# Four places for block 1's compressed rows, and the next pair's second scores, shift and exponential a round sooner

## The chip, the cores and the metric

The kernel runs on one core of a Trainium2 chip. The metric is the device time of one execution in microseconds. Three executions of the kernel before took 2794.94, 2795.05 and 2795.95 us, median 2795.05.

## What is computed

Three transformer blocks run one after the other on 512 tokens of width 1024, all in fp32 (large products are made of two or three products of split operands). Only block 1 is touched: a sparse attention of 16 heads of 64, with three branches, of which this is the part that matters (cut from the reference):

```python
s_c = jnp.einsum('bgrqd,bgnd->bgrqn', qb, k_c).astype(jnp.float32) * scale
p_c = masked_softmax(s_c, c_end[None, :] <= tpos[:, None])
o_c = jnp.einsum('bgrqn,bgnd->bgrqd', p_c.astype(dt), v_c)
...
p_s = masked_softmax(s_s, m_s[:, :, None])
o_s = jnp.einsum('bgrqk,bgqkd->bgrqd', p_s.astype(dt), vs_g)
...
p_w = masked_softmax(s_w, m_w)
o_w = jnp.einsum('bgrqk,bgkd->bgrqd', p_w.astype(dt), vw)
return gb[..., 0:1] * o_c + gb[..., 1:2] * o_s + gb[..., 2:3] * o_w
```

The compressed branch (`s_c`, `p_c`) has 31 keys, so a head has 512 x 31 scores. With 512 tokens the selected and the window branch see all causal keys. The compressed keys come from two small weight matrices, `cw2k` being the second of them (128 x 256 in SBUF), which is used once before the attention.

## The kernel before

TensorE, VectorE, ScalarE, GpSimd and SyncE each have a program written out by hand; they meet at semaphores. Each engine's order of work is that of its program.

The attention of block 1 is one loop of 64 rounds. `head_and_tile(n)` gives round n's head (n // 8 * 2 + n % 2) and its tile of 128 queries (n % 8 // 2): eight rounds make a pair of heads, tiles 0 to 3, the two heads in turn. With m = n // 8, rounds 8m to 8m+7 work on heads 2m and 2m+1, and the compressed rows of heads 2m+2 and 2m+3 are prepared beside them.

TensorE in round n (main loop at L2926): `gate_filler(n)`, three 512-column matmuls for the attention gate (rounds 0 to 47; L2585 to L2587); `scores(n + 1)` (L2856 to L2858), which waits until the exponentials two rounds back are done and, where n % 8 == 5, for `c_shifted`; in rounds 8m and 8m+2 `compressed_scores` of heads 2m+2 and 2m+3 (L2865 the mask, L2868 eight matmuls of 32 columns) into a part of bank 5, waiting for `c_shifted >= h`, that is until the shift of the head before is done; in odd rounds `values(n - 3)` (L2907) for two rounds at once; `transposes(n - 1)` (L2894, and L2891 for the compressed rows where the tile is 0), which waits for the scaled rows and for the copies of the transposes before.

VectorE in round n: `keep_second_pt(n - 2)` copies one branch's transposed rows out of PSUM (L1941) once `tr_done` says they are there; `row_factor(n)` (L1931, L1932) after the exponentials of round n; `maxima(n + 1)` (L1925) after scores(n + 1); in rounds 8m+1 and 8m+3 `compressed_shift` of heads 2m+2 and 2m+3 (a row maximum, L1952, and a subtraction into the compressed rows, L1955); in rounds 8m+4 and 8m+6 `compressed_sum` (L1960 to L1963); once a pair `keep_heads` (L1967).

ScalarE in round n: `keep_pt(n - 2)` copies the other branch's transposed rows (L991, L993); `scale_rows(n)` (L983); in rounds 8m+2 and 8m+4 `compressed_exp` (L997); `exps(n + 1)` (L974); and once a pair, in round 8m+2, the cast of a weight unit (`split_hi`, L589).

GpSimd does taps of the convolution beside the loop (L464 to L469) and the low halves of weight units (L442).

The compressed rows (`PC_ROWS`, seen as `PC`) have two places, one for even and one for odd heads, each of 128 columns: four tiles of 31 scores and one column of zero, cleared once at the start. So the subtraction of head h waits until the rows of head h - 2 have been transposed.

Of the kernel before, what the change touches and what calls it, by code (L numbers as in the profile page):

```python
# [126 lines left out]
def build(nc, t, out, blocks=(1, 2, 3)):  # L127
    ctx = ExitStack()
    FIRST, COUNT, LAST, n_units = plan(blocks)
    with ctx:  # L130
# [119 lines left out]
        CW2K = region(2 * P).rearrange("p (c d) -> p c d", c=2)  # L250
        CW2V = region(2 * DH).rearrange("p (c d) -> p c d", c=2)
        CST = region(4)
# [313 lines left out]
        def _(a):  # L566
# [253 lines left out]
            def block_1():  # L820
# [174 lines left out]
                def compressed_exp(h):  # L995
                    a.wait_ge(c_shifted, h + 1)
                    a.activation(PC[:, h % 2, :, 0:NCMP], PC[:, h % 2, :, 0:NCMP], ACT.Exp).then_inc(c_exp, 1)  # L997
# [5 lines left out]
                for n in range(N + 2):  # L1003
# [6 lines left out]
                    if n % 8 in (2, 4) and n // 8 + 1 < NH // 2:  # L1010
                        compressed_exp(n // 8 * 2 + 2 + (n % 8 == 4))
# [473 lines left out]
        def _(v):  # L1485
            c = Count()

            def link(ins):

                ins.then_inc(dve_step, 1)  # L1490
                v.wait_ge(dve_step, c.add("step"))
# [255 lines left out]
            def block_1():  # L1747
# [199 lines left out]
                def compressed_shift(h):  # L1947

                    v.wait_ge(c_scores, h + 1)
                    at = h % 2 * TT * NC2  # L1950
                    sc = bank[5][:, at:at + TT * NC2].rearrange("p (q n) -> p q n", q=TT)[:, :, 0:NCMP]
                    link(v.tensor_reduce(CST, sc, AX.X, ALU.max))  # L1952
                    if h >= 2:
                        v.wait_ge(tr_done, (h // 2 - 1) * 8 + h % 2 + 1)
                    v.tensor_tensor(PC[:, h % 2, :, 0:NCMP], sc, per_row(CST), ALU.subtract).then_inc(c_shifted, 1)  # L1955

                def compressed_sum(h):
                    to, rows = CMP_FACTOR[:, h % 2], PC[:, h % 2, :, 0:NCMP]
# [20 lines left out]
                for n in range(N + 3):  # L1979
# [6 lines left out]
                    if n // 8 + 1 < NH // 2:  # L1986
                        if n % 8 in (1, 3):
                            compressed_shift(n // 8 * 2 + 2 + (n % 8 == 3))
                        if n % 8 in (4, 6):
                            compressed_sum(n // 8 * 2 + 2 + (n % 8 == 6))  # L1990
# [589 lines left out]
        def _(pe):  # L2580
# [183 lines left out]
            def block_1():  # L2764
# [117 lines left out]
                def transposes(n):  # L2882
# [6 lines left out]
                    if qt == 0:  # L2889
                        pe.wait_ge(c_scaled, h + 1)  # L2890
                        pe.transpose(bank[0][:, P:2 * P], PC_ROWS[:, h % 2], ident)  # L2891
# [34 lines left out]
                for n in range(N + 2):  # L2926
# [4 lines left out]
                    if n % 8 in (0, 2) and n // 8 + 1 < NH // 2:  # L2931
                        compressed_scores(n // 8 * 2 + 2 + (n % 8 == 2))
# [597 lines left out]
```

## Time and profile before

| | us |
|---|---|
| median of three runs | 2795.05 |
| profiled execution, its own time | 2790.86 |
| its span | 2789.1 |
| TensorE busy in the span | 2678.1 (96%) |
| TensorE weight loads | 2195.5 (79%) |
| VectorE busy | 1568.5 (56%) |
| ScalarE busy | 1056.2 (38%) |
| GpSimd busy | 1179.2 (42%) |

All times in the rows are microseconds from the span's start unless marked ns. A timeline row gives its start, its length, the engine, the line, the operation, the result and its operands, and in brackets how long the engine was idle before it and what ended that. Matmuls are pipelined: the listed length is longer than the distance between two starts. The loop of 64 rounds lies between about 275 and 498 us. The granted clock of TensorE is given as a share of 2.4 GHz, its mean over the span is 0.988.

### The profile page before, as it was taken

How to read it: one execution, taken by the hardware profiler on the slowest of the kernel's cores; microseconds unless marked ns; L12 is line 12 of the kernel's file. 1: busy time of each engine (PE TensorE's matmuls, PEld its weight loads, DVE VectorE, ACT ScalarE, POOL GpSimd, SP SyncE). 2: the span in 40 equal slices, each digit the busy share in tenths (PEclk: the TensorE clock that was granted, in tenths of full speed). 3: DMA queues.
4: the chain of work that ended last, by engine and by line, in shares of the span. 5: the costliest groups of instructions: out<-in, count | busy, mean ns of one | idle time of the engine just before them, and what ended most of it. 6: DMA issues, size and time to landing. Idle time of an engine off the chain costs nothing.

```text
span 2789.1 us, 38071 instructions
## 1 busy us (share of the span) xinstructions
PE 2678.1 (96%) x13128; PEld 2195.5 (79%) x13128; DVE 1568.5 (56%) x2448; ACT 1056.2 (38%) x1826; POOL 1179.2 (42%) x592
## 2 busy tenths in 40 slices
PE   8999888999999999999999999999899999999998
PEld 6877777778888878888887788888687778888886
DVE  8996666564342476476656735545623446653364
ACT  4224878623222254443324411112525553211133
POOL 3432595334444444354333344444442224444443
PEclk9999999999999999999999999999999999999999
DMA  3342000233322232221112332222231112322332
GB/s 137 99 140 83 16 24 9 65 131 100 98 98 92 96 131 84 82 94 61 54 38 95 134 98 95 94 98 95 97 104 56 46 45 91 128 97 92 98 98 90
DMA packets 67459, 242.88 MB, mean 87 GB/s; under 512 B 7771, under 2 KB 10116, under 8 KB 66572
## 3 DMA queue, kind: packets, MB, share of 16 engines
q1 hardware_dynamic: 59760, 215.37, 23.7%
q10 hardware_dynamic: 7580, 25.91, 2.7%
q8 instruction: 77, 1.26, 0.2%
q14 instruction: 42, 0.34, 0.0%
HBM read 232.80 MB, written 6.35 MB: 86 GB/s over the span
## 4 chain that ended last, share of the span: by engine, by line
issue 50%; PE 29%; POOL 18%; DVE 1%; ACT 1%; POOLq 1%; DVEq 0%; ACTq 0%
POOL w_lo L442 14%; PE bank L2585 7%; PE bank L2587 7%; PE bank L2586 7%; POOL stat L469 3%; PE bank L3133 2%; PE bank L3122 2%; POOL stat L466 2%; PE bank L2800 1%; POOLq L446 0%; PE bank L2771 0%; PE bank L3106 0%; PE bank L3171 0%; PE bank L3157 0%; PE bank L3109 0%
## 5 line engine op out<-in xcount | busy, mean ns | idle before, releaser
L442 POOL TENSOR_TENSOR w_lo<-raw,w_hi 128x1024 fp32r<-128x1024 f32 x398 | 972.7, 2444 | 1541.7 <-ACT w_hi L589 1420.7
L2585 PE MATMUL bank<-act,w_hi 128*128 128x512 f32 x3128 | 1259.6, 403 | 51.1 <-POOL w_lo L442 15.2
L2587 PE MATMUL bank<-act,w_lo 128*128 128x512 f32 x3128 | 1227.5, 392 | 0.0
L2586 PE MATMUL bank<-act,w_hi 128*128 128x512 f32 x3128 | 1226.3, 392 | 0.0
L589 ACT CAST w_hi<-raw 128x1024 fp32r<-128x1024 f32 x396 | 415.7, 1050 | 898.0 <-PE bank L2587 887.4
L2585 PEld LDWEIGHTS bank<-act,w_hi 128*128 128x128 f32 x3128 | 592.2, 189 | 198.7 <-issue 32.5
L2587 PEld LDWEIGHTS bank<-act,w_lo 128*128 128x128 f32 x3128 | 592.1, 189 | 127.2
L2586 PEld LDWEIGHTS bank<-act,w_hi 128*128 128x128 f32 x3128 | 593.0, 190 | 121.3 <-issue 5.7
L1685 DVE TENSOR_TENSOR X<-X,bank 128x512 f32 x56 | 38.5, 687 | 241.3 <-PE bank L2587 241.3
L2076 DVE CAST act<-tmp 128x512 f32 x64 | 142.5, 2226 | 10.0 <-DVE tmp L2072 5.2
L1837 DVE SCALAR_TENSOR_TENSOR bank<-big,cols,bank 128x512 f32<-128x512 f32 x174 | 117.1, 749 | 0.4
L2907 PE MATMUL bank<-big 128*64 128x128 f32 x768 | 50.7, 283 | 28.7 <-ACT big L991 18.6
L469 POOL TENSOR_TENSOR stat<-stat 128x512 f32<-128x512 f32 x58 | 74.5, 1285 | 4.8
L1732 DVE TENSOR_TENSOR tmp<-bank,stat 128x512 f32<-128x512 f32 x22 | 15.2, 692 | 104.9 <-PE bank L2587 104.9
L2907 PEld LDWEIGHTS bank<-big 128*64 128x64 f32 x768 | 43.0, 140 | 36.4 <-ACT big L991 23.9
L2476 DVE SCALAR_TENSOR_TENSOR big<-bank,stat 128x128 f32<-128x128 f32 (+3 forms) x32 | 15.7, 491 | 92.7 <-ACT stat L1410 92.7
L2251 DVE TENSOR_TENSOR stat<-bank,cst 128x256 f32<-128x256 f32 x96 | 40.7, 425 | 40.4 <-PE bank L3122 38.7
L1713 DVE TENSOR_TENSOR X<-X,bank 128x512 f32<-128x512 f32 x24 | 16.5, 688 | 80.4 <-PE bank L2587 73.9
L3122 PEld LDWEIGHTS bank<-big 128*128 128x128 f32 x384 | 51.2, 194 | 12.3 <-ACT big L1220 4.2
L3122 PE MATMUL bank<-big 128*128 128x128 f32 x384 | 54.2, 282 | 5.5 <-DVE big L2219 3.2
L1925 DVE TENSOR_REDUCE big<-bank 128x2 f32<-128x256 f32 (+3 forms) x64 | 52.5, 820 | 8.8 <-PE bank L2858 7.7
L753 ACT ACTIVATE tmp<-tmp 128x512 f32<-128x512 f32 x24 | 15.2, 631 | 109.0 <-DVE tmp L1729 109.0
(427 smaller groups left out, 2957.6 us busy)
## 6 DMA issues: line engine op xcount, KB each, us to landing
raw<-in_w_dram SPq DMA_DIRECT2D x402, 512.0 KB, 3.4
act_f<-head_rows ACTq DMA_DIRECT2D x8, 768.0 KB, 4.4
proj_rows<-big ACTq DMA_DIRECT2D x4, 1024.0 KB
big<-proj_rows ACTq DMA_DIRECT2D x2, 2048.0 KB, 9.0
X<-in_x_dram SPq DMA_DIRECT2D x4, 512.0 KB, 6.1
act_f<-in_cw1k_dram ACTq DMA_DIRECT2D x4, 512.0 KB, 4.3
cst<-in_consts_dram ACTq DMA_DIRECT2D x2, 648.5 KB, 7.7
X<-big ACTq DMA_DIRECT2D x8, 128.0 KB, 4.0
```

What stands on the lines that cost most here:

```text
L442: pool.tensor_tensor(w_lo[:, u], raw[:, u].rearrange("p (k n) -> p k n", k=KT), w_hi[:, u].bitcast(F32), ALU.subtract).then_inc(w_lo_ready, 1)
L466: pool.tensor_scalar(product, src, w, Z[:, k, 0:1], ALU.mult, ALU.add).then_inc(pool_step, 1)
L469: pool.tensor_tensor(to, acc, product, ALU.add).then_inc(done, 1)
L589: a.copy(w_hi[:, u].rearrange("p k n -> p (k n)"), raw[:, u]).then_inc(w_hi_ready, 1)
L1837: v.scalar_tensor_tensor(acc, src, w, acc, ALU.mult, ALU.add).then_inc(conv_tap, 1)
L2076: v.tensor_copy(hi, y).then_inc(hi_made, 1)
L2585: pe.matmul(o, l_hi, r_hi, start=start, stop=False)
L2586: pe.matmul(o, l_hi, r_lo, start=False, stop=False)
L2587: return pe.matmul(o, l_lo, r_hi, start=False, stop=stop)
L2907: ins = pe.matmul(bank[7][x * DH:x * DH + DH, qt * P:qt * P + P], v_rows, p_cols(x), start=start, stop=stop, tile_position=(0, x * DH), sk ...
L3122: ins = pe.matmul(bank[2 + half][:, quad[j]], MT[:, 2 * half + j], TM[:, 2 * half + j], start=True, stop=True)
L3133: ins = pe.matmul(bank[4 + half][:, quad[j]], XM[:, 2 * half + j], UM[h % 2][:, 2 * half + j], start=True, stop=True)
```

## The change

The compressed rows get four places instead of two: the two of `PC_ROWS` and the two halves of `CW2K`, whose weights have been used by then. Head h uses place h % 4. The zero column of the two new places is cleared by VectorE in the shifts of heads 2 and 3. The subtraction's wait on `tr_done` now concerns head h - 4 and exists from head 4 on.

The second head of the next pair (2m+3) moves: its `compressed_scores` from round 8m+2 to 8m+1 on TensorE, its `compressed_shift` from round 8m+3 to 8m+2 on VectorE, its `compressed_exp` from round 8m+4 to 8m+3 on ScalarE. Its `compressed_sum` stays in round 8m+6, and all of the first head's steps stay in their rounds. The wait of `compressed_scores(h)` for `c_shifted >= h` is as it was.

```diff
--- before.py
+++ after.py
@@ -248,7 +248,13 @@
             return tmp[:, 2 * (n % 3) + j] if n % 3 < 2 else ROWS_3[:, j]
 
         CW2K = region(2 * P).rearrange("p (c d) -> p c d", c=2)
+        PC_ROWS = (PC_ROWS[:, 0], PC_ROWS[:, 1], CW2K[:, 0], CW2K[:, 1])
         CW2V = region(2 * DH).rearrange("p (c d) -> p c d", c=2)
+
+        def compressed_rows(h):
+
+            return PC_ROWS[h % 4].rearrange("p (q n) -> p q n", q=TT)[:, :, 0:NCMP]
+
         CST = region(4)
         CMP_FACTOR = region(8).rearrange("p (b q) -> p b q", b=2)
         MX = region(4).rearrange("p (b k) -> p b k", b=2)
@@ -994,7 +1000,7 @@
 
                 def compressed_exp(h):
                     a.wait_ge(c_shifted, h + 1)
-                    a.activation(PC[:, h % 2, :, 0:NCMP], PC[:, h % 2, :, 0:NCMP], ACT.Exp).then_inc(c_exp, 1)
+                    a.activation(compressed_rows(h), compressed_rows(h), ACT.Exp).then_inc(c_exp, 1)
 
                 compressed_exp(0)
                 compressed_exp(1)
@@ -1007,8 +1013,8 @@
                         scale_rows(n)
                     if n % 8 == 7 and n // 8 < 6:
                         keep_gate(n // 8 + 2, bank[1])
-                    if n % 8 in (2, 4) and n // 8 + 1 < NH // 2:
-                        compressed_exp(n // 8 * 2 + 2 + (n % 8 == 4))
+                    if n % 8 in (2, 3) and n // 8 + 1 < NH // 2:
+                        compressed_exp(n // 8 * 2 + n % 8)
                     if n + 1 < N:
                         exps(n + 1)
                     if 3 <= n < 7:
@@ -1949,13 +1955,15 @@
                     v.wait_ge(c_scores, h + 1)
                     at = h % 2 * TT * NC2
                     sc = bank[5][:, at:at + TT * NC2].rearrange("p (q n) -> p q n", q=TT)[:, :, 0:NCMP]
+                    if h in (2, 3):
+                        link(v.memset(CW2K[:, h - 2].rearrange("p (q n) -> p q n", q=TT)[:, :, NCMP:], 0.0))
                     link(v.tensor_reduce(CST, sc, AX.X, ALU.max))
-                    if h >= 2:
-                        v.wait_ge(tr_done, (h // 2 - 1) * 8 + h % 2 + 1)
-                    v.tensor_tensor(PC[:, h % 2, :, 0:NCMP], sc, per_row(CST), ALU.subtract).then_inc(c_shifted, 1)
+                    if h >= 4:
+                        v.wait_ge(tr_done, (h // 2 - 2) * 8 + h % 2 + 1)
+                    v.tensor_tensor(compressed_rows(h), sc, per_row(CST), ALU.subtract).then_inc(c_shifted, 1)
 
                 def compressed_sum(h):
-                    to, rows = CMP_FACTOR[:, h % 2], PC[:, h % 2, :, 0:NCMP]
+                    to, rows = CMP_FACTOR[:, h % 2], compressed_rows(h)
                     v.wait_ge(c_exp, h + 1)
                     link(v.tensor_reduce(to, rows, AX.X, ALU.add))
                     link(v.reciprocal(to, to))
@@ -1984,8 +1992,8 @@
                     if n + 1 < N:
                         maxima(n + 1)
                     if n // 8 + 1 < NH // 2:
-                        if n % 8 in (1, 3):
-                            compressed_shift(n // 8 * 2 + 2 + (n % 8 == 3))
+                        if n % 8 in (1, 2):
+                            compressed_shift(n // 8 * 2 + n % 8 + 1)
                         if n % 8 in (4, 6):
                             compressed_sum(n // 8 * 2 + 2 + (n % 8 == 6))
                     if 4 <= n < 8:
@@ -2888,7 +2896,7 @@
                         pe.wait_ge(c_kept, n // 8 * 2 + n % 8)
                     if qt == 0:
                         pe.wait_ge(c_scaled, h + 1)
-                        pe.transpose(bank[0][:, P:2 * P], PC_ROWS[:, h % 2], ident)
+                        pe.transpose(bank[0][:, P:2 * P], PC_ROWS[h % 4], ident)
                     for j in range(2):
                         for k in range(qt + 1):
                             ins = pe.transpose(bank[6 * j][:, k * P:k * P + P], probabilities(n, j)[:, k * P:k * P + P], ident)
@@ -2928,8 +2936,8 @@
                         gate_filler(n)
                     if n + 1 < N:
                         scores(n + 1)
-                    if n % 8 in (0, 2) and n // 8 + 1 < NH // 2:
-                        compressed_scores(n // 8 * 2 + 2 + (n % 8 == 2))
+                    if n % 8 in (0, 1) and n // 8 + 1 < NH // 2:
+                        compressed_scores(n // 8 * 2 + 2 + n % 8)
                     if n % 2 and n >= 3:
                         values(n - 3)
                     if 1 <= n <= N:
```

## Rows read from the trace of the kernel before

**Rows 1.** Windows: length, busy us of PE, PEld, DVE, ACT, POOL; clock; DMA.

```profile
272.00:498.00 226.00, 190.87 (x1644) 163.23 (x1646) 147.85 (x373) 175.92 (x502) 140.85 (x129) 0.98 0.05 17
```

**Rows 2.** Waits, 272 to 490 us: engine line <- released by: us, times, longest.

```profile
DVE big L1941 <- PE bank L2894: 35.7, 30, 2.5
...
DVE big L1955 <- PE bank L2894: 10.8, 6, 2.1
```

**Rows 3.** Timeline of TensorE, rounds 9 to 11.

```profile
310.28 0.48 PE L2585 MATMUL bank<-act,w_hi 128*128 128x512 f32 x1
...
311.51 0.28 PE L2858 MATMUL bank<-big_r 128*128 128x256 f32 x1
311.72 2.19 PE L2907 MATMUL bank<-big 128*64 128x128 f32 x36
313.84 0.33 PE L2891 MATMUL bank<-cst,big 128*128 128x128 f32 x1
...
315.49 0.22 PE L2865 MATMUL bank<-big_r 128*128 128x128 f32 x1
...
316.41 0.33 PE L2891 MATMUL bank<-cst,big 128*128 128x128 f32 x1
...
318.80 0.88 PE L2907 MATMUL bank<-big 128*64 128x128 f32 x12 [0.34 <-ACT big L991]
```

**Rows 4.** Timeline of VectorE, rounds 9 and 10.

```profile
311.83 0.69 DVE L1925 TENSOR_REDUCE big<-bank 128x2 f32<-128x512 f32 x1 [0.31 <-PE bank L2858]
312.44 0.28 DVE L1952 TENSOR_REDUCE big<-bank 128x4 f32<-128x124 f32 x1
314.49 0.29 DVE L1955 TENSOR_TENSOR big<-bank,big 128x124 f32<-128x124 f32 x1 [1.78 <-PE bank L2894]
314.69 0.28 DVE L1941 COPY big<-bank 128x128 f32<-128x128 f32 x1
```

**Rows 5.** Timeline of ScalarE, rounds 10 and 11.

```profile
314.42 0.27 ACT L991 COPY big<-bank 128x128 f32<-128x128 f32 x1 [0.84 <-PE bank L2894]
...
317.33 1.04 ACT L589 CAST w_hi<-raw 128x1024 fp32r<-128x1024 f32 x1
318.27 0.27 ACT L991 COPY big<-bank 128x128 f32<-128x128 f32 x1
```

**Rows 6.** Timeline of TensorE, then VectorE, round 41.

```profile
421.96 0.28 PE L2858 MATMUL bank<-big_r 128*128 128x256 f32 x1
...
422.88 0.28 DVE L1952 TENSOR_REDUCE big<-bank 128x4 f32<-128x124 f32 x1
```

**Rows 7.** Timeline of TensorE, rounds 1 and 2.

```profile
279.24 0.27 PE L2858 MATMUL bank<-big_r 128*128 128x256 f32 x1
280.68 0.47 PE L2891 MATMUL bank<-cst,big 128*128 128x128 f32 x1 [1.17 <-ACT tmp L983]
...
281.23 0.78 PE L2585 MATMUL bank<-act,w_hi 128*128 128x512 f32 x1
```

**Rows 8.** Timeline of VectorE, round 1.

```profile
281.35 0.17 DVE L1931 RECIPROCAL big<-big 128x2 f32<-128x2 f32 x1 [1.12 <-ACT tmp L974]
...
282.54 0.29 DVE L1955 TENSOR_TENSOR big<-bank,big 128x124 f32<-128x124 f32 x1
```

**Rows 9.** Windows around two low clocks, columns as in rows 1.

```profile
281.00:284.00 3.00, 3.00 (x11) 2.52 (x10) 1.97 (x9) 2.47 (x11) 0.00 (x0) 0.50 0.00 0
...
306.00:309.00 3.00, 3.00 (x18) 2.77 (x16) 1.31 (x4) 1.25 (x3) 2.75 (x3) 0.66 0.02 5
```

**Rows 10.** Timeline of TensorE, rounds 49 and 52.

```profile
448.05 1.20 PE L2907 MATMUL bank<-big 128*64 128x128 f32 x18 [0.20 <-DVE big L1941]
...
456.49 0.47 PE L2856 MATMUL bank<-act,big_r 128*128 128x512 f32 x1 [0.99 <-DVE big L1955]
```

**Rows 11.** One line's instructions: ns min/median/max, first and last start.

```profile
L1932 DVE TENSOR_TENSOR big<-big x64: 160/161/2225, 279.7 to 489.1; 128x2 f32<-128x2 f32 x64
```

**Rows 12.** Chain that ended last, behind the last conv tap: start, us, what.

```profile
457.26 39.81 issue
```

## The prediction

> **What bounds the kernel now.** I read the busy time of the stretch in which the attention loop of block 1 runs, then who waits for whom, then the timelines of TensorE, VectorE and ScalarE side by side around one change of head pair. Over the 226 us of the loop TensorE is busy for 190.87 us, ScalarE for 175.92 and VectorE for 147.85 [rows 1]. No engine is full, so the loop runs at the pace of a ring: scores (TensorE), row maxima (VectorE), exponentials (ScalarE), row factor (VectorE), scaling (ScalarE), transposes (TensorE), copies of the transposed rows, values. The reader should see in [rows 3] that TensorE has no idle time from scores(10) to transposes(9), and in [rows 2, 4, 5] that the two others wait for it there. VectorE idles 1.78 us before the subtraction of L1955, ScalarE 0.84 us before the copy of L991, both until transposes(8) are done. So in rounds 8m+1 and 8m+2 TensorE's order of work sets the time. POOL is not in it: once its share of the convolution is done it is idle for 39.81 us, until ScalarE's first cast behind the loop [rows 12].
>
> I number rounds by n, with m = n // 8. Heads 2m+2 and 2m+3 are the next pair.
>
> **The order that the change makes.** In round 8m+1 TensorE does the gate's three matmuls, scores(8m+2), now compressed_scores(2m+3), then values(8m-2), then transposes(8m). compressed_scores(h) waits for c_shifted >= h, here the shift of head 2m+2. VectorE does that shift in the same round, behind maxima(8m+2), which in turn waits for the scores(8m+2) that TensorE has only just issued. So the wait can never be met on arrival. Before, it stood in round 8m+2, behind two more matmul groups.
>
> **Cost of the stall.** In round 9, scores(10) end where values(6) begin, 311.72 [rows 3]. maxima(10) begin at 311.83, the reduce of L1952 at 312.44 and takes 0.28 [rows 4]. The subtraction no longer waits for transposes(8), so it follows after about 0.03 and takes its 0.29: done at 313.04. TensorE stands still for 313.04 - 311.72 = 1.32 us. Queued behind it are values(6) and transposes(8). The pair of round 41 is alike: its last scores matmul begins at 421.96 (that of round 9 at 311.51) and its reduce at 422.88, that is 0.92 later against 0.93 [rows 3, 4, 6]; the three pairs between lie within 0.25 us of this.
>
> **Cost of the moved matmuls.** compressed_scores(5) hold TensorE from 315.49 to 316.41 in round 10, 0.92 us [rows 3]. There they are covered: what ScalarE needs from round 10 is scores(11), ahead of them, and its copy of transposes(9) comes only at 318.27, 1.86 us after these began, behind exps(11) and a weight cast [rows 5]. In round 9 they lie ahead of transposes(8), for which both others wait. So transposes(8) and scores(11) come 1.32 + 0.92 = 2.24 us later.
>
> **What comes back.** TensorE itself gets 0.92 us back in round 10, but the next thing it needs, values(8), waits for ScalarE's copy at 318.27 and was already 0.34 us idle for it [rows 3]. ScalarE's chain copy(8), scale(10), exps(11), cast, copy(9) has only small waits in it [rows 5] and starts at 314.42 + 2.24. So the whole ring is 2.24 us later, and the 0.92 becomes idle time. The subtraction after transposes(8) goes, and the copy of L1941 behind it starts 0.20 us sooner (314.49 to 314.69 [rows 4]), but exps(11) also wait for maxima(11), and these for scores(11), which are the full 2.24 late; I take 0. In round 8m+3 VectorE loses 0.28 + 0.29 of shift, which mostly fell into time that it then spent waiting for transposes [rows 2]: 0. The shift goes into round 8m+2, ahead of the copy of transposes(8m+1); that copy then comes about 0.57 later again, still under ScalarE's 1.04 us cast [rows 5]. ScalarE's compressed_exp of the odd head moves one round: 0. Two memsets of four columns are on no path except that of head 2 in round 1; the nearest row, VectorE's smallest operation, takes 0.16 us [rows 11], so with its step's wait I take 0.2 there. They can't gain anything. Five full pairs (m = 1 to 5): 5 x 2.24 = 11.2 us.
>
> **The first pair (m = 0)** has no values(-2) and a worse wait. The last scores(2) matmul begins at 279.24; transposes(0) waited 1.17 us for ScalarE and began at 280.68 [rows 7]. VectorE comes to the shift of head 2 only after row_factor(1) at 281.35, which waits for ScalarE, and subtracts at 282.54 [rows 8]. With the memset c_shifted comes at 282.54 + 0.29 + 0.2 = 283.0. The compressed scores then take 0.92 to 1.2 us, and transposes(0) begin near 284.1, 3.4 later. Before, the next filler and scores ran at 0.50 of full clock [rows 9], so they cost about twice the 1.44 us of round 9 (310.28 to 311.72 [rows 3]); the same is likely again. About 0.2 is absorbed since ScalarE was just behind, and 0.92 no longer follows. Bounds 1.8 and 3.1; I take 2.7, near the upper one, since TensorE idles longer than before.
>
> **The last pair (m = 6)** has no gate matmuls. The stall and the moved work cost 2.3 as before (0.20 us of idle before values(46) is taken up by it). But TensorE then waited 0.99 us in round 52 for the second shift, L1955 [rows 10]; that shift is now a round sooner and the wait goes: 2.3 - 1.0 = 1.3.
>
> **Sum.** 2.7 + 11.2 + 1.3 = 15.2 us. What follows the loop is a chain led by TensorE and fed by it, so it shifts as a whole. Against the profiled execution's own 2790.86 us (span 2789.1) that is 2806.1; the median of the runs is 2795.05, 4.2 above it, and the forecast goes by the median: 2810.3 us.
>
> **Jitter.** The 2-element product of L1932 takes 0.161 us in the middle and 2.225 at most [rows 11], depending on what GpSimd does at that moment, and ScalarE waits for it. A shifted loop meets GpSimd at other points, for about 3 us either way in sum.
>
> **Rivals.** (a) Only TensorE's own loss counts: the 0.92 us comes back since ScalarE keeps pace. Then 5 x 1.32 = 6.6, the first pair 1.8, the last 0.3: 8.7, giving 2803.8. Against it: ScalarE's copy at 318.27 already held values(8) up. (b) The clock. Of the stretches around 281 and 306 the rows show 0.50 and 0.66 of full clock, the lower of TensorE's two levels (1.2 against 2.4 GHz) for part of them [rows 9]. Each new stall may set off another such stretch; 3 us at 0.66 lose 1.0 us of full-speed work, 3 us at 0.50 lose 1.5. In all five pairs: 5 to 7.5 more, 2815 to 2818. The Trainium skill, "TensorE: Matmul & The Clock Gate", section "What's actually happening", says that an idle TensorE is put back to half clock and has to be busy for a while to leave it, which speaks for (b). (c) Faster: the ring gains the 0.57 us of shift that leaves VectorE's round 8m+3 in seven pairs and the 0.99 of the last: 4.0 + 1.0 = 5.0, 2790.1. It decides only from the point where TensorE gets to the moved matmuls after the subtraction is done, so where it had at least 1.3 us of idle before values(8m-2); rows show none in round 9 and 0.20 in round 49 [rows 3, 10]. (d) The stall costs nothing because TensorE takes the ready matmuls of values(8m-2) past the waiting ones, or slack absorbs it: 2795 to 2799. Against it: at 280.68 transposes(0) waited 1.17 us, and the gate matmul of the next round, which needed nothing from it, started only behind it at 281.23 [rows 7]. The Trainium skill says the same on that page, section "Step-by-step: what each phase is for": only weight loads are pulled ahead, matmuls keep program order; by it (d) would be 0.
>
> **How the numbers follow.** Chances: forecast with its jitter (2806 to 2814) 0.62; (a) 0.14; (b) 0.12; (d) 0.07; (c) 0.05. A measurement of this kernel can tell about 0.2%, 5.6 us, so slower begins at 2800.6. Slower takes the forecast, (b) and nearly all of (a): 0.87. Same: (d) and the rest of (a), 0.08. Faster: (c), 0.05. The range 2800 to 2820 takes in forecast, (a) and (b) with jitter and leaves out (c) and (d).
>
> **What would show it.** In the changed profile: a TensorE wait for L1955 ahead of L2865, seven times, 1.3 us each (over 3 in round 1), 10 to 12 us in sum; the 10.8 us of VectorE idle before L1955 [rows 2] gone, but a like amount before L1941; 1.2 us of idle before values(8) in place of 0.34; the loop's end 15 us later; everything behind it of equal length. I would be wrong if values(8m-2) ran before the compressed scores, if the copy of L991 in round 8m+3 came under 2 us later in its round, or if stretches after the loop changed length.

## The result

The changed kernel takes 2819.44 us (median of 4 runs, 2815.45 to 2822.94), the kernel before 2794.99 us (median of 4 runs). The ratio is 1.009, with a 95% interval of 1.0078 to 1.0102: slower by 22 to 29 us. The forecast was 2810.3. Its sign holds, and so does the part of its mechanism that is about the order of work on TensorE. The other 9 us have a cause of their own, which the sum had at nothing: a lower TensorE clock behind the new wait.

The profiled execution of the changed kernel took 2815.45 us, with a span of 2813.7, 24.6 above that of the kernel before. Both profiles lie about 4 us below their medians, so their difference can be used. In the changed kernel's source all lines behind the new ones are shifted: L1955 is now L1963, L1941 is L1947, L1925 is L1931, L1932 is L1938, L991 is L997, L2865 is L2873, L2868 is L2876, L2907 is L2915, L2891 is L2899, L2894 is L2902.

Who waits for whom in the loop (us in total, times, longest), over 272 to 517 us, which holds the same rounds as 272 to 490 us in [rows 2]:

```profile
DVE big L1947 <- PE bank L2902: 71.0, 36, 7.1
...
PE bank L2873 <- DVE big L1963: 12.4, 8, 2.9
```

VectorE's wait ahead of the subtraction is gone, and its wait for transposes ahead of the copy has grown from 35.7 to 71.0 us, more than the 10.8 us that the forecast moved there. New is TensorE's wait for the subtraction ahead of the compressed scores (line L2873), 12.4 us in 8 times; one of them, 0.77 us ahead of the loop, is there before too. This wait is the stall that the forecast named.

TensorE in round 9, against [rows 3]:

```profile
316.18 0.28 PE L2866 MATMUL bank<-big_r 128*128 128x256 f32 x1
317.87 0.33 PE L2873 MATMUL bank<-big_r 128*128 128x128 f32 x1 [1.42 <-DVE big L1963]
318.03 1.35 PE L2876 MATMUL bank<-big_r 128*128 128x32 f32 x8
319.31 3.46 PE L2915 MATMUL bank<-big 128*64 128x128 f32 x36
322.70 0.33 PE L2899 MATMUL bank<-cst,big 128*128 128x128 f32 x1
...
327.69 0.88 PE L2915 MATMUL bank<-big 128*64 128x128 f32 x12 [1.32 <-ACT big L999]
```

The stall is there (1.42 us idle), the moved matmuls stand behind it, values and transposes behind them, and values(8) now wait 1.32 us for ScalarE instead of 0.34. But there is a row that the forecast did not have: the 36 matmuls of values(6) take 3.46 us, against 2.19 before. Below are the same rows of round 25, and then three windows around it (columns as in [rows 1], the clock third from the end):

```profile
378.38 0.33 PE L2873 MATMUL bank<-big_r 128*128 128x128 f32 x1 [1.52 <-DVE big L1963]
378.54 1.01 PE L2876 MATMUL bank<-big_r 128*128 128x32 f32 x8
379.48 3.67 PE L2915 MATMUL bank<-big 128*64 128x128 f32 x36
```

```profile
378.00:384.00 6.00, 5.62 (x50) 5.22 (x51) 0.49 (x3) 1.06 (x6) 5.43 (x7) 0.72 0.00 0
378.40:379.90 1.50, 1.50 (x17) 1.47 (x19) 0.00 (x0) 0.46 (x3) 1.40 (x2) 1.00 0.00 0
380.10:383.30 3.20, 3.20 (x31) 2.87 (x28) 0.00 (x0) 0.00 (x0) 2.93 (x4) 0.50 0.00 0
```

The granted clock is 0.72 over these 6 us, a mixture of the two levels, 1.2 and 2.4 GHz. It was still 1.00 while the narrow matmuls ran and fell to 0.50 only under the values, over 1.5 us after the stall had ended. The values of this round take 3.46, 2.19, 3.67, 3.80, 3.66 and 4.11 us in the six pairs that have them, so the clock was low in five of six. The one that kept it, in round 17, has the same order and the same idle time ahead of it:

```profile
348.93 0.33 PE L2873 MATMUL bank<-big_r 128*128 128x128 f32 x1 [1.51 <-DVE big L1963]
...
350.04 2.19 PE L2915 MATMUL bank<-big 128*64 128x128 f32 x36
```

Over the stretch of [rows 1]:

```profile
272.00:498.00 226.00, 185.83 (x1448) 159.32 (x1448) 135.90 (x345) 155.10 (x448) 139.84 (x128) 0.92 0.05 17
```

The clock is 0.92 against 0.98 there. (The loop now ends at 525.6 us; over all of it the clock is 0.92 too.)

**Where the 24.6 us lie**, by the starts of the transposes of rounds 8m+1 (L2891, L2899):

| stretch | before | changed | difference | forecast |
|---|---|---|---|---|
| to the first (m = 0) | 280.68 | 287.20 | 6.5 | |
| first to second | 33.16 | 35.50 | 2.3 | both together 4.9 |
| five intervals, m = 1 to 6 | 136.33 | 155.45 | 19.1 | 11.3 |
| m = 6 to 7 | 24.28 | 23.34 | -0.9 | -1.0 |
| to the end of the loop (first unit behind it) | 23.92 | 24.07 | 0.2 | 0 |
| behind the loop | 2290.7 | 2288.1 | -2.6 | 0 |

The five intervals hold the stalls of m = 2 to 6 (four times 2.24 and once 2.3 in the forecast) and are free of the start and the end; I call them the five pairs and use them to compare kernels below.

Two rows of the table need not be wholly the change's doing. In the first, the changed kernel's clock is low from 274 us on, some ten microseconds ahead of its first stall. The kernel of the experiments that has the old order on TensorE and only the shift and the exponential sooner shows the same. First the changed kernel, then that one:

```profile
274.00:280.00 6.00, 5.31 (x22) 5.02 (x23) 3.24 (x13) 1.42 (x6) 0.00 (x0) 0.51 0.00 0
```

```profile
275.50:285.50 10.00, 10.00 (x37) 8.94 (x37) 6.08 (x26) 4.37 (x19) 0.00 (x0) 0.50 0.00 0
```

That other kernel reaches its first transposes at 283.35 us, 2.7 later than the kernel before, with nothing on TensorE changed. In the last row, two stretches of low clock in the profile of before have no counterpart in the changed one, where the clock is 1.00 over 1235 to 1247 and 2120 to 2132 us:

```profile
1210.00:1222.00 12.00, 8.66 (x47) 7.37 (x45) 10.10 (x19) 3.57 (x6) 7.72 (x6) 0.86 0.46 144
2096.00:2108.00 12.00, 10.07 (x44) 8.10 (x43) 2.85 (x7) 7.11 (x19) 2.39 (x1) 0.86 0.25 87
```

Against GpSimd's weight units the shift between the two profiles falls from 27.2 to 26.0 us by the first of them and from 26.3 to 24.6 us at the second.

One stall is twice as long. In round 49 VectorE's row factor (L1938) took 1.47 us while GpSimd made a low half of a weight unit, and it ended within 0.02 us of it. First GpSimd's row, then VectorE's, then TensorE's:

```profile
468.55 2.35 POOL L448 TENSOR_TENSOR w_lo<-raw,w_hi 128x1024 fp32r<-128x1024 f32 x1
```

```profile
469.45 1.47 DVE L1938 TENSOR_TENSOR big<-big 128x2 f32<-128x2 f32 x1
470.85 0.68 DVE L1931 TENSOR_REDUCE big<-bank 128x2 f32<-128x512 f32 x1
471.45 0.27 DVE L1960 TENSOR_REDUCE big<-bank 128x4 f32<-128x124 f32 x1
471.75 0.29 DVE L1963 TENSOR_TENSOR big<-bank,big 128x124 f32<-128x124 f32 x1
```

```profile
472.09 0.46 PE L2873 MATMUL bank<-big_r 128*128 128x128 f32 x1 [2.90 <-DVE big L1963]
```

TensorE now waits for everything that stands in VectorE's queue ahead of the shift, and so takes over VectorE's delays: 2.90 us here, where kernels with a row factor of 0.16 us show 1.59. That GpSimd is the cause is borne out by all 64 row factors of this profile: the 31 that took over 0.25 us all ended within 0.02 us of an operation of GpSimd, and the 26 that met none took 0.16 us each.

### The profile page after: what moved, and what is told of

It reads as the page before. It is cut to its first block, busy times and chain, and to the rows that moved or that the text cites. A ratio compares the mean times of both kernels' runs of the same rounds, so it can differ in the third digit from the quotient of the medians.

```text
span 2813.7 us, 38071 instructions
## 1 busy us (share of the span) xinstructions
PE 2690.6 (96%) x13128; PEld 2206.1 (78%) x13128; DVE 1568.3 (56%) x2450; ACT 1055.3 (38%) x1826; POOL 1179.1 (42%) x592
## 4 chain that ended last, share of the span: by engine, by line
issue 50%; PE 31%; POOL 15%; DVE 2%; ACT 2%; POOLq 1%; DVEq 0%; ACTq 0%
POOL w_lo L448 13%; PE bank L2593 7%; PE bank L2595 7%; PE bank L2594 7%; PE bank L3141 2%; PE bank L3130 2%; POOL stat L475 1%; PE bank L2915 1%; POOL stat L472 1%; PE bank L2808 1%; PE bank L2876 0%; PE bank L2902 0%; POOLq L452 0%; ACT tmp L980 0%; PE bank L2779 0%
## 5 line engine op out<-in xcount | busy, mean ns | idle before, releaser
L2915 PE MATMUL bank<-big 128*64 128x128 f32 x768 | 58.1, 310 | 29.7 <-ACT big L997 17.0
L2915 PEld LDWEIGHTS bank<-big 128*64 128x64 f32 x768 | 50.0, 157 | 36.0 <-ACT big L997 31.1
L1947 DVE COPY big<-bank 128x128 f32<-128x128 f32 (+3 forms) x64 | 31.2, 487 | 76.8 <-PE bank L2902 76.7
L1738 DVE TENSOR_TENSOR tmp<-bank,stat 128x512 f32<-128x512 f32 x22 | 15.2, 691 | 104.9 <-PE bank L2595 104.9
L1931 DVE TENSOR_REDUCE big<-bank 128x2 f32<-128x256 f32 (+3 forms) x64 | 52.4, 818 | 8.5 <-PE bank L2866 7.5
```

The costliest lines, as they stand in the source:

```text
L1931: v.tensor_reduce(MX[:, b], score_branches(n), AX.XY, ALU.max, negate=True).then_inc(neg_ready, 1)
L2915: ins = pe.matmul(bank[7][x * DH:x * DH + DH, qt * P:qt * P + P], v_rows, p_cols(x), start=start, stop=stop, tile_position=(0, x * DH), sk ...
```

## The experiments

The ratio is to the kernel before, in brackets its 95% interval. "Five pairs" is from one profile of each; kernels with the old order on TensorE and the clock up agree there within 0.1 us (136.33 before, and 136.38, 136.30 and 136.24 in kernels below). Diffs are against the changed kernel unless said otherwise. "Idle matmuls" are matmuls whose result nobody reads. "Values" without a number are the 36 matmuls of round 8m+1, 2.19 us at the full clock.

### The matmuls behind the transposes, or between

```diff
+if n % 8 == 0 and n // 8 + 1 < NH // 2:
+    compressed_scores(n // 8 * 2 + 2)
-if n % 8 in (0, 1) and n // 8 + 1 < NH // 2:
-    compressed_scores(n // 8 * 2 + 2 + n % 8)
 if n % 2 and n >= 3:
     values(n - 3)
 if 1 <= n <= N:
     transposes(n - 1)
+if n % 8 == 1 and n // 8 + 1 < NH // 2:
+    compressed_scores(n // 8 * 2 + 3)
```

> The whole change, but the moved compressed_scores of the odd head stand behind transposes(8m) in round 8m+1 instead of ahead of values(8m-2). Theory A (the order on TensorE is all of the loss: a wait for VectorE's shift ahead of values and transposes): VectorE has done the shift long before TensorE gets there, so no wait before these matmuls, and the time is that of the kernel before, 2795 within 4 us. Theory B (the four places, the memsets, or the earlier shift and exponential on VectorE and ScalarE cost): stays at 2812 or above.

Measured: 2800.96 us, 1.0025 (1.0015 to 1.0035), five pairs 141.32. The second kernel has the same edit with the last two lines between values and transposes:

> The whole change, but the moved compressed_scores stand between values(8m-2) and transposes(8m): the 2.1 us of values cover VectorE's shift, so the stall goes, and 0.92 us of matmuls still lie ahead of transposes(8m) (the first pair has no values and keeps its stall). Theory A: only the moved work is left, 6 x 0.9 plus 3 to 5 for the first pair, some 2803 (2800 to 2806), clock in the loop near 0.97. Theory C (the stall matters little, the matmuls ahead of transposes(8m) are what costs): 2812 or above.

Measured: 2801.10 us, 1.0029 (1.0018 to 1.0040), five pairs 142.87, with low clock in one of them. Moving nothing but these matmuls past values takes two thirds of the loss away, so B and C fall. But the run behind the transposes was expected at 2795 and is 6 above. There the matmuls no longer delay transposes(8m), but they now stand ahead of the gate's matmuls and scores(8m+3), which before ran ahead of them. Five pairs differ by 5.0 and 6.5 us from 136.33, so the matmuls' 0.92 us lie on the path in either place. Their old place in round 8m+2, behind the scores, was the covered one.

### The parts off TensorE

```diff
 # e1: all three steps of the odd head in their old rounds, four places
-if n % 8 in (0, 1) and n // 8 + 1 < NH // 2:
-    compressed_scores(n // 8 * 2 + 2 + n % 8)
+if n % 8 in (0, 2) and n // 8 + 1 < NH // 2:
+    compressed_scores(n // 8 * 2 + 2 + (n % 8 == 2))
...
 # e9: only this edit; shift and exponential stay a round sooner
```

> Four places for the compressed rows (with the two memsets and the relaxed wait), every step in its old round. Theory A (order on TensorE plus low clock is all): the subtraction no longer waits for the transposes and the copy behind it starts 0.2 us sooner, nothing waits for it: 2795 within 2 us. Theory B (the places themselves cost, which would explain the 6 us that are left when the moved matmuls stand behind the transposes): 2800.

> The change without its part on TensorE: the odd head's compressed_scores stay in round 8m+2, its shift moves to round 8m+2 on VectorE and its exponential to 8m+3 on ScalarE. Theory A: 2795 to 2797. Theory E (the shift ahead of keep_heads and the copy of transposes(8m+1) on VectorE delays TensorE's values(8m), and is the 6 us left in the run with the matmuls behind the transposes): 2799 to 2802, with more TensorE idle before values in round 8m+3.

Measured: four places alone 2792.39 us, 0.9992 (0.9983 to 1.0001); with shift and exponential a round sooner 2792.24 us, 0.9991 (0.9982 to 0.9999). B and E fall; the forecast's zeros for places, memsets, shift and exponential are right, if anything these parts gain 2 to 3 us (the intervals reach from -5 to 0). All of the loss is in the third part, TensorE's.

### The moved matmuls without the stall

compressed_scores waits for the shift of the even head since both heads' scores lie in bank 5 of PSUM, the memory that TensorE writes. With the odd head's in bank 3, which is free in that round, this wait can go. Instead scores(8m+4), which use bank 3 again, have to wait for the odd head's shift:

```diff
-if h:
+if h == 1 or h % 2 == 0 and h:
     pe.wait_ge(c_shifted, h)
+to = bank[3 if h % 2 and h > 1 else 5]     # and in compressed_shift
...
 # scores(n), which reuses bank 3
-if n % 8 == 5 and h + 1 < NH:
-    pe.wait_ge(c_shifted, h + 3)
+if n % 8 == 4 and h + 2 < NH:
+    pe.wait_ge(c_shifted, h + 4)
```

> The change with the odd head's compressed scores in PSUM bank 3, free in that round, instead of bank 5 where the even head's are: they need no longer wait until the even head's were read. So TensorE does them in the same place as in the change but without the stall. Theory A: only 0.92 us of moved work ahead of transposes(8m) per pair, clock near that of the kernel before: 2795 + 6 = 2801 (2798 to 2804). If the loss were in the moved work or in the earlier shift: 2812 or above.

Measured: 2799.52 us, 1.0018 (1.0009 to 1.0027), five pairs 141.19, no low clock in them. Round 25:

```profile
369.08 0.28 PE L2866 MATMUL bank<-big_r 128*128 128x256 f32 x1
369.20 0.22 PE L2874 MATMUL bank<-big_r 128*128 128x128 f32 x1
369.26 1.01 PE L2877 MATMUL bank<-big_r 128*128 128x32 f32 x8
370.20 2.19 PE L2916 MATMUL bank<-big 128*64 128x128 f32 x36
```

The same matmuls in the same place, no idle time ahead of them, values at 2.19. The moved work costs 141.19 - 136.33 = 4.9 us in five pairs, 0.97 each; the forecast said 0.92. The new wait of scores(8m+4) was met late in three rounds (0.35, 0.35 and 1.49 us, the last behind the five pairs), and what it costs is inside these numbers. The stall and what follows it make the other 14.3.

### The stall alone

```diff
 # on the kernel with four places and the old order
 if n % 8 in (0, 2) and n // 8 + 1 < NH // 2:
     compressed_scores(n // 8 * 2 + 2 + (n % 8 == 2))
+if n % 8 == 1 and n // 8 + 1 < NH // 2:
+    pe.wait_ge(c_shifted, n // 8 * 2 + 3)
```

> Four places, but everything else in the order of the kernel before; only TensorE waits in round 8m+1, ahead of values(8m-2), for the shift of head 2m+2. No work is moved: the stall alone. Theory A: 1.3 to 1.5 us in six pairs and 2 to 3 in the first, 10 to 12 us, and with the clock going down behind it up to 18: 2806 to 2813. If the stall does nothing by itself: 2795. If the clock theory D is right the loop's granted clock falls below 0.96 here too.

Measured: 2804.03 us, 1.0031 (1.0019 to 1.0043), five pairs 141.90: 5.6 above before, 1.1 per stall (forecast 1.32). Values in round 25:

```profile
374.62 0.28 PE L2866 MATMUL bank<-big_r 128*128 128x256 f32 x1
376.19 2.19 PE L2915 MATMUL bank<-big 128*64 128x128 f32 x36 [1.30 <-DVE big L1963]
```

1.30 us idle, and full clock behind it, as in four of the other pairs (1.30 to 1.59 us idle). The exception is round 9, where a slow row factor made the stall longer:

```profile
318.07 3.75 PE L2915 MATMUL bank<-big 128*64 128x128 f32 x36 [2.00 <-DVE big L1963]
```

So with values right behind it a stall of up to 1.6 us left the clock alone in five of five pairs, and the one of 2.00 us did not. Filled with idle matmuls:

```diff
 if n % 8 == 1 and n // 8 + 1 < NH // 2:
+    for _ in range(10):
+        pe.matmul(bank[3][:, 0:2 * P], IDENT_R, CAUSAL_2R, start=True, stop=True)
     pe.wait_ge(c_shifted, n // 8 * 2 + 3)
```

> The stall without moved work, filled with the same ten idle matmuls (result unused) as in the filled run of the whole change. Theory D (what a stall costs is mostly the low clock behind it): about 5 us less than the unfilled stall's 2804, 2797 to 2801. Rival (in this ring the length of the stall counts): 2803 to 2805.

Measured: 2801.77 us, 1.0030 (1.0019 to 1.0041), five pairs 141.88 against 141.90. Where the clock was up anyway, filling changes nothing, so idle matmuls are no gain by themselves. D, which expected 5 us less here, fails for this kernel.

### The change with its stall filled

```diff
+if h % 2 and h > 1:
+    for _ in range(10):
+        pe.matmul(bank[3][:, 0:2 * P], IDENT_R, CAUSAL_2R, start=True, stop=True)
 if h:
     pe.wait_ge(c_shifted, h)
```

> The whole change, with ten idle matmuls of 256 columns into a bank that nobody reads ahead of the wait in round 8m+1; they take about 1.2 us, so TensorE waits about as long as before for the shift but is at work while it waits. Their result is not used. Theory D (half or more of what the forecast missed is the low clock that follows the stall): granted clock of the loop back from 0.92 to 0.96 or more, values(8m-2) back to 2.2 us each, 2808 to 2813 us. Rival (the low clock is beside the path, or the length of the stall is all that counts): clock may rise, time stays at 2818 to 2822.

Measured: 2802.36 us, 1.0036 (1.0022 to 1.0050). Round 25:

```profile
371.89 0.28 PE L2866 MATMUL bank<-big_r 128*128 128x256 f32 x1
372.01 1.36 PE L2872 MATMUL bank<-big_r 128*128 128x256 f32 x10
373.65 0.33 PE L2876 MATMUL bank<-big_r 128*128 128x128 f32 x1 [0.28 <-DVE big L1963]
373.82 1.01 PE L2879 MATMUL bank<-big_r 128*128 128x32 f32 x8
374.76 2.19 PE L2918 MATMUL bank<-big 128*64 128x128 f32 x36
```

```profile
372.00:378.00 6.00, 5.72 (x64) 5.17 (x63) 2.07 (x7) 2.06 (x8) 5.44 (x7) 1.00 0.01 4
```

The compressed scores still come 1.76 us behind the last matmul of the scores ahead of them, about as late as in the change (1.69 in round 9), but TensorE is at work in between. The clock is 1.00, values take 2.19 us in all six pairs, and the kernel is 17 us faster than the change by the medians, 15 by the two ratios. Five pairs take 145.44 against 155.45. This is the missing piece: of the five pairs' 19.1 us, 10.0 go with the filling. About 1.3 of the 10.0 are the slow row factor of round 49, which this profile does not have, so some 8.7 are low clock, in four of the five pairs. The kernel came out 6 us better than D expected.

### What sets the low clock off

A stall alone did it once in six pairs, with 2.00 us of idle time; the moved matmuls alone never. Both together did it in five. To tell whether the narrow matmuls (32 columns each) behind the stall matter, idle copies of them were put behind the stall of the stall-only kernel:

```diff
     pe.wait_ge(c_shifted, n // 8 * 2 + 3)
+    for _ in range(8):
+        pe.matmul(bank[3][:, 0:NC2], IDENT_R, CMP_MASK_R[:, 0:NC2], start=True, stop=True)
```

> The stall-only kernel, with eight idle matmuls of 32 columns (result unused) right behind the stall, as the change has its eight there; the real ones stay in round 8m+2. Theory F (the stall together with the narrow matmuls behind it brings the clock down): values(8m-2) take 3.4 us or more in at least three of six pairs, five pairs take 150 us or more, 2812 or above. Rival (narrow matmuls don't matter; what the change's place does otherwise): all values at 2.2, five pairs 145 to 147 us, 2806 to 2809.

Measured: 2818.91 us, 1.0092 (1.0075 to 1.0109); its profile is its fastest run (2811.6), with five pairs at 149.97 and values at 3.85, 3.74, 3.60, 3.58, 2.19, 2.19. Round 25:

```profile
379.21 1.27 PE L2944 MATMUL bank<-big_r 128*128 128x32 f32 x8 [1.49 <-DVE big L1963]
380.41 3.60 PE L2915 MATMUL bank<-big 128*64 128x128 f32 x36
```

Low in four of six, one of them behind 2.00 us of idle time as in the stall-only kernel and three behind 1.30 to 1.49. F holds by the count of pairs, though its 150 us was missed by 0.03. All four runs support it: they lie at 2811.6 to 2819.2 us against 2799.8 to 2804.7 of the stall-only kernel, and their granted clocks are 0.982 to 0.986 against 0.985 to 0.987. The added matmuls hold TensorE for about 1 us a pair, 7 in all, of the 15 between the medians. Then half of the filling (range(5) in place of range(10)):

> The whole change with only five idle matmuls (result unused) in the stall: TensorE idles about 0.8 us instead of 1.4, the stall is as long. Theory G (the idle time counts by its length): values(8m-2) at 2.2 us in most pairs, five pairs 145 to 148 us, 2802 to 2807. If any idle time with the narrow matmuls behind is enough: five pairs 152 us or more, 2814 or above.

Measured: 2807.32 us, 1.0052 (1.0033 to 1.0071), five pairs 147.07; values take 2.19 us in five pairs and 3.85 in one, that of round 17. G holds for the count of low stretches. But the low one had 0.88 us of idle time ahead of it, and that of round 9, with 1.43, kept the clock, so the idle time next to it does not decide alone. And the ten idle matmuls behind the moved ones instead of ahead:

```diff
+if n % 8 == 1 and n // 8 + 1 < NH // 2:
+    for _ in range(10):
+        pe.matmul(bank[3][:, 0:2 * P], IDENT_R, CAUSAL_2R, start=True, stop=True)
 if n % 2 and n >= 3:
     values(n - 3)
```

> The whole change with the ten idle matmuls behind the moved compressed_scores, ahead of values(8m-2), so the stall is idle as in the change and 1.2 us of work is added to the path. Theory F/G (idle plus narrow matmuls lower the clock): the clock has fallen or not before the extra work runs, so five pairs take 155 to 165 us, 2824 or above. If what counts is how much TensorE does over a longer stretch: the added work keeps the clock up, five pairs about 145.4 + 6 = 151, 2810 to 2816.

Measured: 2821.08 us, 1.0104 (1.0087 to 1.0121), five pairs 153.99; values at 2.19 in five pairs and 3.06 in the last. Neither side came out cleanly: the clock stays up in five pairs although the stall is idle and the narrow matmuls follow it, which speaks against F in its strict form, but the median lies between the two sides, nearer to F's. 153.99 is 8.5 above the filled kernel. By interval the difference is 1.31, 1.28, 1.25, 1.80 and 2.91 us: in the first three it is the idle matmuls, which now lie wholly on the path, and the last has the low clock in it. The 0.5 us more in the fourth are not explained.

A long idle time needs no narrow matmuls. The kernel before has one, ahead of the values of round 7, with the lower clock behind it:

```profile
303.27 2.02 PE L2907 MATMUL bank<-big 128*64 128x128 f32 x28 [2.50 <-ACT big L991]
304.70:308.00 3.30, 3.30 (x17) 2.78 (x14) 0.94 (x3) 1.64 (x6) 2.63 (x3) 0.50 0.00 0
```

Two others in the same trace, 2.29 us at 353.02 and 2.10 us at 387.98, have full clock behind them. So neither the length of the idle time nor what follows it is enough to say whether the clock falls. A rival that no run here tested is the moment at which the idle time comes.

### A longer stall

```diff
 link(v.tensor_reduce(CST, sc, AX.X, ALU.max))
+if h % 2 == 0 and h:
+    for _ in range(4):
+        link(v.tensor_reduce(CST, sc, AX.X, ALU.max))
```

> The whole change with four more reductions of the same scores on VectorE ahead of each even head's subtraction (results as before): the stall grows by 4 x 0.31 = 1.2 us in each of seven pairs, to about 2.7. If the stall's length passes on in full: 7 x 1.2 = 8.7 more than the changed kernel's 2819, 2828. If slack takes part of a stall of this kind (as the filled run suggests): under 4 more, 2819 to 2823. If low clock grows with it: above 2830, loop clock under 0.90.

Measured: 2830.89 us, 1.0138 (1.0123 to 1.0154), five pairs 162.58. Against the change that is 11.5 us more (13 by the ratios), over the full length of the added stall. The low clock grew with it: values take 4.11 us in four pairs, 3.43 in one and 2.19 in one, and the clock over 272 to 498 us is 0.89. In round 9 it had fallen before the stall of 2.69 us ended at 319.55, so before any narrow matmul:

```profile
319.10:319.50 0.40, 0.00 (x0) 0.00 (x0) 0.36 (x2) 0.00 (x0) 0.30 (x2) 0.50 0.00 0
```

Filled with twenty idle matmuls:

> The doubled stall (2.7 us), filled with twenty idle matmuls (result unused). Unfilled it took 162.6 us for five pairs and 2831. If all beyond the filled single stall (145.4) was its 1.2 us each: five pairs 151.5 us, 2811 to 2815. If filling only works for short stalls: 157 or more.

Measured: 2815.98 us, 1.0080 (1.0064 to 1.0097), five pairs 152.49, all values at 2.19. Round 25:

```profile
378.25 0.28 PE L2869 MATMUL bank<-big_r 128*128 128x256 f32 x1
378.37 2.56 PE L2875 MATMUL bank<-big_r 128*128 128x256 f32 x20
381.30 0.33 PE L2879 MATMUL bank<-big_r 128*128 128x128 f32 x1 [0.37 <-DVE big L1966]
381.47 1.01 PE L2882 MATMUL bank<-big_r 128*128 128x32 f32 x8
382.41 2.19 PE L2921 MATMUL bank<-big 128*64 128x128 f32 x36
```

From the first idle matmul to the compressed scores it is 2.93 us here and 1.64 in the filled single stall, 1.29 more. Five pairs are 7.05 longer, 1.41 each, so the added part of the stall passes on in full. From no stall (141.19) to the single one (145.44) it was only 0.85 a pair for about 1.5 us of stall; that the other half microsecond or so fell into slack of the ring is argued from these sums and not shown by rows. Filling takes 10 us off the single stall's five pairs and 10 off the doubled one's.

### Two tries at something faster

scores(n+1) ahead of the gate's matmuls, on the change and on the kernel before:

```diff
-if n < 6 * KT:
-    gate_filler(n)
 if n + 1 < N:
     scores(n + 1)
+if n < 6 * KT:
+    gate_filler(n)
```

> The change with scores(n+1) ahead of the gate's three matmuls in every round. The maxima, and behind them the shift, start 0.78 us sooner against TensorE's own order, so the stall falls from 1.4 to about 0.65 us in six pairs. If the low clock follows the length of the idle time (theory D): it mostly goes, loop clock 0.96 or more, 2805 or below, lower still if sooner scores help the ring in other rounds. If the stall's existence alone sets it off: clock stays at 0.92, 2814.

Measured: 2809.01 us, 1.0053 (1.0038 to 1.0067), five pairs 150.40. The stalls are 0.89 to 1.59 us rather than 0.65, since VectorE then comes to the maxima late, behind a copy and a row factor (in round 17 the last matmul of the scores starts at 339.51 and the maxima at 340.66), and four of six pairs still have low clock. The gain on the change is 10 us by the medians where at least 14 were expected.

> The kernel before with scores(n+1) ahead of the gate's three matmuls in every round. In the rounds in which TensorE waits for ScalarE the maxima and exponentials then come up to 0.78 us sooner; in the others nothing waits for it. 2788 to 2795; if it delays transposes through waits for exponentials that now come ahead of ready gate matmuls: 2797 to 2802.

Measured: 2795.68 us, 1.0006 (0.9997 to 1.0015): no difference. The last one filled TensorE's idle time elsewhere, on the kernel with only VectorE's and ScalarE's parts of the change:

```diff
+if n == 1 or n % 8 == 7:
+    for _ in range(8):
+        pe.matmul(bank[3][:, 0:2 * P], IDENT_R, CAUSAL_2R, start=True, stop=True)
 if n % 2 and n >= 3:
     values(n - 3)
```

> The change without its part on TensorE (2792), with eight idle matmuls of 256 columns (0.9 us, result unused) ahead of values in the last round of every pair and ahead of the first transposes, where TensorE idles 1.2 to 2.5 us for ScalarE. Theory D: the few low-clock stretches of the loop (some 6 us of full-speed work lost) shrink, 2788 to 2792. If the matmuls lie on the path: 2794 to 2799.

Measured: 2792.00 us, 0.9989 (0.9980 to 0.9998), against 0.9991 without it. Five pairs 136.24; there was no low clock in those pairs to remove. Ahead of them there was: in the kernel without the filling the clock is 0.50 behind the idle time of round 7 (306.3 to 309.5 us), and here it is 1.00 (303 to 313 us), with 30.17 us from the first transposes to the second instead of 32.57. Four of the eleven runs take 2786.4 to 2788.0 us, less than any run of any other kernel, the other seven 2791.7 to 2792.7, so the median hides a gain of 4 us that comes in some executions only. The fastest kernels of the study are this one and the one without it, 2 to 3 us below the kernel before by their medians, hardly more than the measurement can tell.

## Why the prediction was right and wrong

**What bounds the kernel, and the order.** Right. TensorE's own order in rounds 8m+1 and 8m+2 sets the time, and the wait is never met on arrival: 1.42, 1.51, 1.52, 1.29 and 1.50 us of idle time in rounds 9 to 41 against 1.32, and 2.90 in round 49. That TensorE's matmuls would not pass the waiting ones (rival d) is shown: values(6) start behind the compressed scores.

**The moved matmuls.** Right, 0.97 against 0.92 us a pair by the kernel with the other bank. That they were covered in their old place follows from this kernel and from the two that put them elsewhere: none of three other places was free. Rival (a), in which they come back, falls.

**The stall.** Somewhat too large: alone 1.1 us a pair, on top of the moved work 0.85, against 1.32. With the clock kept up the change costs 9.1 us in five pairs instead of the 11.3 of the sum.

**The parts off TensorE.** Right at zero, within the measurement.

**The low clock: the step that failed.** In the sum it stood at nothing for every pair behind the first. It was rival (b), with a chance of 0.12 and a price of 5 to 7.5 us. Measured are some 8.7 us in five pairs, about 2.2 for each of the four with low clock, so the rival was priced too low as well; in the whole kernel the filling takes 15 to 17 us off. The prediction gives no row against (b). The trace of before had rows for both sides: idle times of 2.29 and 2.10 us ahead of values with full clock behind them, and one of 2.50 us with the lower clock, in round 7. None of them had narrow matmuls behind it, and with those 1.3 to 1.5 us of idle time were often enough, as the run with idle narrow matmuls shows. Per pair the low clock costs about 1.5 us in values alone (3.67 against 2.19). The Trainium skill, "TensorE: Matmul & The Clock Gate", section "What's actually happening", says that the clock follows how busy TensorE was recently. The trace agrees in kind: the five falls in rounds 9 to 49 of the changed kernel come 0.1 to 1.6 us after the end of an idle time of 1.3 to 2.9 us.

**The first pair.** Its bounds were 1.8 to 3.1 us. To the second transposes, where the forecast makes 2.7 + 2.2 = 4.9, the difference is 8.9 us; with the stalls filled it is 4.2 (318.08 against 313.84). Here too the clock is low, 0.50 from 274 to 291 us, but it fell ahead of the first stall, as it did in a kernel with the old order on TensorE, which is 2.1 us late at the second transposes (315.93). So a part of the 4.0 us above the forecast, about 2, may be chance and not the change; a single profile can't part them. The wait of round 1 was 1.45 us and not over 3, since TensorE at the lower clock came to it later; in three kernels whose clock fell only from 283 or 284 us it was 3.54 or 3.55.

**The last pair.** The wait of 0.99 us in round 52 went, as forecast (-0.9), but the stall of 2.90 us, inherited from VectorE's row factor, was not in the sum. The 2.225 us maximum of that operation [rows 11] was booked as jitter in both directions; ahead of a new wait of TensorE it only adds, 1.3 us here.

**Sum.** The forecast's 15.2 stands against 24.6 between the profiles. The kernel with its stall filled, which is what the sum described, comes out 11.1 above the kernel before between profiles, and 1.0036 by its runs, 6 to 14 us. So the order was slightly overpriced and the clock left out. The loop alone took 27.2 us longer in the profile, and the stretch behind it 2.6 less, where the forecast had equal length. Most of the 2.6 are the two low stretches of before at 1216 and 2100 us; that is luck of the two executions that were profiled.

**Open.** How idle time, narrow matmuls and the work around them combine. Rounds 17 and 25 of the changed kernel have the same rows and the same 1.5 us of idle time, and only the second lost the clock; whether the moment counts was not tested. That low clock makes the missing microseconds is shown by the filling; what exactly sets it off is not.

## What to carry to other kernels

Before moving work on TensorE past a wait, find what the producer has ahead of it in its own queue: a wait placed right behind the matmuls that feed it can't be met on arrival, and it inherits every delay of the other engine's queue. Price the stall together with the granted clock: where narrow matmuls followed an idle time of 1.3 to 1.5 us, the wide work behind often ran at the lower level, and that cost more than the stall itself (2.2 us against 0.85 to 1.1). If the wait only guards a shared PSUM bank, another bank removes it, at the price of a wait where that bank is used next.

## What the runs showed of the hardware

- With values right behind it a stall of 1.3 to 1.6 us lowered the clock in none of five pairs, and one of 2.00 us did. With eight matmuls of 32 columns in between, stalls of 1.3 to 1.5 us did so in four of five pairs of the changed kernel and in three of five (1.30 to 1.59 us) of the kernel with idle copies of them. Ten idle matmuls of 256 columns in the stall prevented it in all six pairs, five of them in five of six.
- The clock fell up to 1.6 us after the idle time had ended: in round 25 of the changed kernel it was 1.00 under the narrow matmuls and 0.50 under the values behind them.
- At the lower level 36 matmuls took 4.11 us instead of 2.19.
- Idle matmuls had no effect on time where the clock was up (141.88 against 141.90 us over five pairs).
- A product of two elements a row on VectorE took 0.16 us when GpSimd was at rest and up to 1.47 us in the changed kernel when it was not; all 31 slow ones ended within 0.02 us of a GpSimd operation.
